# Gate and up products of the feed-forwards as 256-column products, high weights 128 bytes further on

## The reference

```python
def swiglu(x, w_in, w_out):
    gu = x @ w_in
    g, u = jnp.split(gu, 2, axis=-1)
    return (jax.nn.silu(g) * u) @ w_out
...
        x = x + 0.5 * swiglu(rms_norm(x, ffn1_norm[l]), ffn1_w_in[l], ffn1_w_out[l])
```

## Time and profile before

| | |
|---|---|
| median of 3 runs | 2235.34 us (2235.04 to 2235.49) |
| span of the profiled execution | 2233.4 us |
| around the span (median less span) | 1.9 us |
| TensorE busy | 2227.1 us, 100% of the span, granted clock 1.000 |
| VectorE busy | 1833.4 us, 82% |
| ScalarE busy | 1131.6 us, 51% |
| DMA | 53% of 16 engines' span |

### The profile page before, as it was taken

One profiled execution on the slowest core, in us unless ns is written; L12 is line 12 of the kernel. 1 busy time (PEld: TensorE's weight loads), 2 busy tenths in 40 slices (PEclk: granted clock), 3 DMA queues, 4 the chain that ended last, 5 costly groups with the idle time before them and its releaser, 6 DMA issues.

```text
span 2233.4 us, 42466 instructions
## 1 busy us (share of the span) xinstructions
PE 2227.1 (100%) x16140; PEld 2051.0 (92%) x16140; DVE 1833.4 (82%) x3023; ACT 1131.6 (51%) x1503; POOL 4.8 (0%) x10
## 2 busy tenths in 40 slices
PE   9999999999999999999999999999999999999999
PEld 8998999999998999999999889999999998999998
DVE  8888568888888668887988878888898887888887
ACT  5445465445445565444434676654454446766443
POOL 0000000000000000000000000000000000000000
PEclk9999999999999999999999999999999999999999
DMA  7555445555555435654556443555556555344654
GB/s 253 193 194 208 159 153 198 197 196 171 199 196 207 170 135 189 213 194 163 202 190 206 170 152 125 179 197 190 188 177 207 189 174 189 120 142 166 221 196 133
DMA packets 76817, 407.63 MB, mean 183 GB/s; under 512 B 9264, under 2 KB 9920, under 8 KB 44336
## 3 DMA queue, kind: packets, MB, share of 16 engines
q1 hardware_dynamic: 75792, 404.93, 53.0%
q10 hardware_dynamic: 720, 0.89, 0.1%
q0 software_dynamic: 208, 0.49, 0.1%
HBM read 405.23 MB, written 1.05 MB: 182 GB/s over the span
## 4 chain that ended last, share of the span: by engine, by line
PE 97%; DVE 1%; issue 0%; ACT 0%; DMA 0%; DVEq 0%; SPq 0%; ACTq 0%
PE ps_proj L684 13%; PE ps_aux L693 13%; PE ps_y L263 10%; PE ps_y L264 10%; PE ps_y L265 10%; PE ps_proj L688 7%; PE ps_aux L696 7%; PE ps_proj L1120 4%; PE ps_proj L1127 4%; PE ps_proj L1121 4%; PE ps_proj L263 2%; PE ps_proj L265 1%; PE ps_proj L264 1%; PE ps_aux L651 1%; PE ps_proj L651 1%; PE ps_aux L1941 1%
## 5 line engine op out<-in xcount | busy, mean ns | idle before, releaser
L130 DVE TENSOR_TENSOR w_lo_front<-w_raw_front,w_hi_front 128x2048 fp32r<-128x2048 f32 x238 | 544.0, 2286 | 42.3 <-ACT w_hi_front L105 42.0
L105 ACT CAST w_hi_front<-w_raw_front 128x2048 fp32r<-128x2048 f32 x238 | 452.9, 1903 | 178.0 <-PE ps_aux L696 144.8
L263 PE MATMUL ps_y<-hidden_lo,w_hi_back 128*128 128x256 f32 x1344 | 372.5, 277 | 0.1
L264 PE MATMUL ps_y<-hidden_hi,w_lo_back 128*128 128x256 f32 x1344 | 371.3, 276 | 0.0
L265 PE MATMUL ps_y<-hidden_hi,w_hi_back 128*128 128x256 f32 x1344 | 371.3, 276 | 0.0
L105 ACT CAST w_hi_back<-w_raw_back 128x1024 fp32r<-128x1024 f32 x248 | 259.8, 1048 | 146.4 <-PE ps_y L265 119.8
L887 ACT ACTIVATE silu_gate<-silu_gate 128x256 f32<-128x256 f32 x176 | 73.7, 419 | 508.6 <-DVE silu_gate L924 508.5
L684 PE MATMUL ps_proj<-xt_lo_hi,w_hi_front 128*128 128x512 f32 x1280 | 319.7, 392 | 0.0
L693 PE MATMUL ps_aux<-xt_lo_hi,w_hi_front 128*128 128x512 f32 x1280 | 319.6, 392 | 0.0
L130 DVE TENSOR_TENSOR w_lo_back<-w_raw_back,w_hi_back 128x1024 fp32r<-128x1024 f32 x248 | 302.2, 1218 | 4.0 <-ACT w_hi_back L105 3.3
L684 PEld LDWEIGHTS ps_proj<-xt_lo_hi,w_hi_front 128*128 128x128 f32 x1280 | 228.5, 188 | 39.6
(11 more groups left out here) (462 smaller groups left out, 3826.5 us busy)
## 6 DMA issues: line engine op xcount, KB each, us to landing
w_raw_front<-in_stream SPq DMA_DIRECT2D x251, 1024.0 KB, 4.9
w_raw_back<-in_stream SPq DMA_DIRECT2D x252, 512.0 KB, 3.7
m_rel_bias<-in_rel_bias SPq DMA_DIRECT2D x2, 2048.0 KB, 8.2
m_params<-in_params SPq DMA_DIRECT2D x2, 656.0 KB, 4.2
w_raw_front<-in_stream SPq DMA_DIRECT2D x4, 256.0 KB, 6.6
w_raw_front<-in_stream SPq DMA_DIRECT2D x2, 512.0 KB, 8.8
x<-in_x ACTq DMA_DIRECT2D x3, 256.0 KB, 6.7
out<-x SPq DMA_DIRECT2D x3, 256.0 KB, 2.3
```

Source lines behind the costliest of these rows:

```text
L105: self.nc.scalar.copy(self.hi[part][:, parity], self.raw[part][:, parity]).then_inc(self.hi_done[part], by)
L130: eng.tensor_tensor(self.lo[part][:, parity], self.raw[part][:, parity], self.hi[part][:, parity].bitcast(F32), ALU.subtract).then_inc(sel ...
L263: nc.tensor.matmul(out, ah, bl, start=start, stop=False)
L264: nc.tensor.matmul(out, al, bh, start=False, stop=False)
```

## The change

- All gate and up products have 256 columns and write the first half of their bank. A 512-column product becomes two, with the low and then the high part of the activations, each with its own load of the same 128 x 128 weights (`both_high`).
- In `ffn_up`, both gate and up are a run of 16 products on the high weights, then 8 on the low ones. PE's first wait there is now for the low weights (`split`), not for the high ones.
- In `ffn_first` and `ffn_start` the products of a block k are `all_three` (high x low, low x high, high x high) in turn.
- VectorE no longer adds halves: in a step it scales straight from PSUM; for the first slot of a feed-forward it copies the bank out (`first_out`) and scales with the rows of PSUM (`first_scale`).
- `w_hi_front` starts 128 bytes further on (the gap ahead of it has 72 floats, the gap behind it is gone). Every other buffer stays at its address.

```diff
-        sb("gap_hi_front", [P, 40], F32)
+        sb("gap_hi_front", [P, 72], F32)
         self.hi = [sb("w_hi_front", [P, 2, 2 * CH], F32R)]
-        sb("gap_hi_back", [P, 32], F32)
...
+def all_three(s, bank, part, k, stop=True):
+    hi, lo = part
+    cols = slice(k * P, (k + 1) * P)
+    out = bank[:, 0:T]
+    s.nc.tensor.matmul(out, hi[:, cols], s.xl[:, k], start=k == 0, stop=False)
+    s.nc.tensor.matmul(out, lo[:, cols], s.xh[:, k], start=False, stop=False)
+    return s.nc.tensor.matmul(out, hi[:, cols], s.xh[:, k], start=False,
+                              stop=stop and k == KD - 1)
+def both_high(s, bank, part, k, stop=False):
+    hi = part[0][:, k * P:(k + 1) * P]
+    s.nc.tensor.matmul(bank[:, 0:T], hi, s.xl[:, k], start=k == 0, stop=False)
+    return s.nc.tensor.matmul(bank[:, 0:T], hi, s.xh[:, k], start=False, stop=stop)
...
     pe = s.nc.tensor
-    gate, bank = w.parts(slot, 0), s.pj[slot % 2]
-    pe.wait_ge(w.hi_done[0], base + slot + 1)
-    for k in range(KD):
-        s.nc.tensor.matmul(bank[:], gate[0][:, k * P:(k + 1) * P],
-                           s.xlh[:, k].rearrange("p j t -> p (j t)"), start=k == 0, stop=False)
     pe.wait_ge(w.split[0], base + slot + 3)
...
+    for c, bank in enumerate((s.pj[slot % 2], s.pa[slot % 2])):
+        part = w.parts(slot, c)
+        for k in range(KD):
+            both_high(s, bank, part, k)
+        for k in range(KD):
+            last = high_low(s, bank, part, k)
+        w.taken(last, c)
...
-        for bank, part in three:
-            both_high(s, bank, part, k)
-        last_gate = high_low(s, s.pj[0], gate0, k)
+        last_gate = all_three(s, s.pj[0], gate0, k)
...
-    def add_gate(before, k):
+    def first_out(to, bank, c, done):
+        w.wait_taken(dve, base, slot0, c)
+        nc.vector.tensor_copy(to[:, 0], bank[:, 0:T]).then_inc(done, 1)
+    def first_scale(of, came, done):
+        dve.wait_ge(came, f + 1)
+        nc.vector.tensor_tensor(of[:, 0], of[:, 0], s.py[1][:, 0:T], ALU.mult).then_inc(done, 1)
+    def scale_gate(before, k):
+        p = k % 2
         w.wait_taken(dve, base + before, slot0 + k, 0)
+        nc.vector.tensor_tensor(s.act[:, p], s.pj[p][:, 0:T], s.rbc[:], ALU.mult).then_inc(
+            s.gate_scaled, 1)
```

More of the change, by code:

```diff
@@ L666, in by_high @@
     cols = slice(k * P, (k + 1) * P)
-    nc.tensor.matmul(bank[:, T:2 * T], hi[:, cols], s.xh[:, k], start=k == 0, stop=False)
+    nc.tensor.matmul(bank[:, 0:T], hi[:, cols], s.xh[:, k], start=k == 0, stop=False)
     nc.tensor.matmul(bank[:, 0:T], lo[:, cols], s.xh[:, k], start=False, stop=False)
@@ L680, in ffn_up @@
     pe = s.nc.tensor
-    gate, bank = w.parts(slot, 0), s.pj[slot % 2]
-    pe.wait_ge(w.hi_done[0], base + slot + 1)
-    for k in range(KD):
-        s.nc.tensor.matmul(bank[:], gate[0][:, k * P:(k + 1) * P],
-                           s.xlh[:, k].rearrange("p j t -> p (j t)"), start=k == 0, stop=False)
-    pe.wait_ge(w.split[0], base + slot + 3)
[L687 to L698, removed]
+    pe.wait_ge(w.split[0], base + slot + 3)
+    for c, bank in enumerate((s.pj[slot % 2], s.pa[slot % 2])):
[5 more added lines that the diff above has]
+        w.taken(last, c)
 def ffn_first(s, w, base, slot0, n):
@@ L721, in ffn_first @@
         wait_x(s, n, k)
-        for bank, part in three:
-            both_high(s, bank, part, k)
-        last_gate = high_low(s, s.pj[0], gate0, k)
-        last_up = high_low(s, s.pa[0], up0, k)
-        last = high_low(s, s.pj[1], gate1, k)
+        last_gate = all_three(s, s.pj[0], gate0, k)
+        last_up = all_three(s, s.pa[0], up0, k)
+        last = all_three(s, s.pj[1], gate1, k)
         if k == KD - 1:
@@ L768, in ffn_start @@
     gate1, up1 = w.parts(1, 0), w.parts(1, 1)
[L770 to L776, removed]
     for _ in range(WARM):
@@ L782, in ffn_start @@
         wait_x(s, 0, k)
-        high(s.pj[0], gate0, k)
+        both_high(s, s.pj[0], gate0, k)
     pe.wait_ge(s.lead_lo, 1)
     for k in range(2):
-        low(s.pj[0], gate0, k)
+        high_low(s, s.pj[0], gate0, k)
     for k in range(2, 4):
         wait_x(s, 0, k)
-        by_both(s, s.pj[0], gate0, k)
+        all_three(s, s.pj[0], gate0, k)
     pe.wait_ge(s.lead_lo, 2)
     for k in range(4):
-        by_both(s, s.pa[0], up0, k)
+        all_three(s, s.pa[0], up0, k)
     pe.wait_ge(s.lead_lo, 3)
@@ L804, in ffn_start @@
     for k in range(KD):
-        high(s.pj[1], gate1, k)
+        both_high(s, s.pj[1], gate1, k)
     pe.wait_ge(s.half_split, HALF_AT[0] + 1)
     for k in range(KD):
-        last = low(s.pj[1], gate1, k)
+        last = high_low(s, s.pj[1], gate1, k)
     w.taken(last, 0)
@@ L812, in ffn_start @@
     for k in range(KD):
-        high(s.pa[1], up1, k)
+        both_high(s, s.pa[1], up1, k)
     pe.wait_ge(s.ident_rounded, 1)
@@ L817, in ffn_start @@
     for k in range(KD):
-        last = low(s.pa[1], up1, k)
+        last = high_low(s, s.pa[1], up1, k)
     w.taken(last, 1)
@@ L913, in ffn_vector, with scale_up @@
     c0 = f * FC
-    def add_gate(before, k):
+    def first_out(to, bank, c, done):
[6 more added lines that the diff above has]
+        p = k % 2
         w.wait_taken(dve, base + before, slot0 + k, 0)
+        nc.vector.tensor_tensor(s.act[:, p], s.pj[p][:, 0:T], s.rbc[:], ALU.mult).then_inc(
+            s.gate_scaled, 1)
+    def scale_up(before, k):
         p = k % 2
[L918 to L927, removed]
-        w.wait_taken(dve, base + before, slot0 + k, 1)
[L929 to L936, removed]
+        w.wait_taken(dve, base + before, slot0 + k, 1)
+        nc.vector.tensor_tensor(s.hid[:, p], s.pa[p][:, 0:T], s.rbc[:], ALU.mult).then_inc(
+            s.up_scaled, 1)
     def hidden(before, k):
@@ L988, in ffn_vector @@
         inverse(s, n)
-    add_gate(0, 0)
-    add_up(0, 0)
+    first_out(s.act, s.pj[0], 0, s.gate_added)
+    first_out(s.hid, s.pa[0], 1, s.up_added)
     dve.wait_ge(s.rows_done, spread_count(n))
-    scale_gate(0, 0, s.py[1][:, 0:T])
-    scale_up(0, 0, s.py[1][:, 0:T])
+    first_scale(s.act, s.gate_added, s.gate_scaled)
+    first_scale(s.hid, s.up_added, s.up_scaled)
     hidden(0, 0)
```

23 lines of the change are left out of this document (4 added, 19 removed).

## The result

Before 2235.06 us, after 2238.74 us (medians of 20 executions each); the ratio, which goes by the means (2235.03 and 2239.67), is 1.0021, with a 95% interval of 1.0013 to 1.0029. I had forecast 2223.2 us and faster. One execution of after, 3706.76 us long at a lower clock, is left out of the ratio.

A forecast was written before the change was run, and what follows sets the result against it. TensorE, busy for the whole span, was taken to bound the kernel. Loops 8.5, waits 2.8 and openings 0.8 made 12.1 us off 2233.4, 2221.3, plus 1.9 for the runs' median: 2223.2 us, range 2219 to 2246.

The forecast's parts named there:

- Cost per product at the fast pace: Steady feed-forward loop: 72 narrow products at 113.33 ns make a slot 8.160 us against 8.213, 8.5 us less in all.
- third rival: All products: a fixed cost that the split doubles makes loops 6.4 us longer, 2239 us; chance 0.05, shared with small losses.
- Waits at the loops' ends: First and last down of each loop: TensorE's waits for VectorE shrink, 2.8 us saved, bounds 0 and 3.5.
- Openings: `ffn_first` and `ffn_start`: cheaper split products 0.5 us, three first downs no longer slow 0.3; 0.8 us saved.
- The wait moved ahead. ... nothing: Gate's low front weights needed 1.8 us sooner but made 6.1 us ahead, so the earlier wait costs nothing.
- Second, alignment: Reason for the fast pace in the loops: all four weight buffers now lie alike, front taking back's favourable alignment.
- Third, once fast, the streams stay fast: Reason for the fast pace in the loops: fast streams in this alignment stay fast at changes of weight buffer.
- First, the state in which the loop is entered: Reason for the fast pace: in six of eight feed-forwards the opening's restart turns fast after four slow products.
- Slow is a state that can last: Reason against the fast pace: 6 of 14 down runs restarted behind a wait stayed slow through all 24 products.
- some loops slow, 0.20: Rival: some feed-forward loops run slow, 6.6 us each; one gives 2229.8, two 2236.4, three 2243 us; chance 0.20.
- Mixers: Mixers' projections, whose front high weights move too: taken as 0 us, bounds -3 and +3.
- all loops slow: Rival: slow pace in all feed-forward loops, +44 us less the savings on waits, about 2277 us; chance 0.12.

The follow-up runs named there:

- e3: Kernel after with the low-weights wait put back behind the gate's high products and the old gaps before and behind w_hi_front: 2223.12 us, ratio 0.9945.
- e7: Kernel before with only the loop's eight wide gate and up products made 16 narrow ones, VectorE still adding halves: 2227.73 us, ratio 0.9968.
- e2: Kernel after with the old gaps, so the front's high weights 128 bytes back; waits as in after: 2229.82 us, ratio 0.9975.
- e6: Kernel after, low-weights wait back behind the high products, both low weight buffers and everything behind them 128 bytes further: 2226.81 us, ratio 0.9964.
- e4: Kernel before with only the new gaps, wide products kept: 2245.73 us, ratio 1.0047.
- e1: Kernel after with the wait for the low weights put back behind the gate's high products: 2243.73 us, ratio 1.0035.
- e5: Kernel after, low-weights wait back behind the high products, all moving operands 128 bytes further, weight buffers still alike: 2250.59 us, ratio 1.0081.
- e9: Kernel after, low-weights wait back behind the high products, both back weight buffers 128 bytes apart (modulo 512) from both front ones: 2222.20 us, ratio 0.9942.
- e10: As e3, but front's high weights 128 bytes on the other side of the other buffers, modulo 512 (gaps of 104 and 96 floats): 2223.24 us, ratio 0.9946.
- e8: As e3, but front's high weights 64 bytes from the other buffers instead of 128 (gaps of 56 and 16 floats): 2296.55 us, ratio 1.0276.

## Why the prediction was wrong

*Cost per product at the fast pace*: right. 8.160 us a slot was forecast, and 8.160 is what every fast loop shows; the loops of e3 are 8.6 us shorter than before over 19 slots each, where I had 8.5 over 20. A slow loop costs 6.5 (6.1 in these 19 slots, 0.4 in the first slot and the last down) where I had 6.6. My third rival, a fixed cost that the split doubles (2239), came near the measured time for the wrong reason: e7 doubles the products and gains 7 us. With it falls the use that I made of the Trainium skill, TensorE: Matmul & The Clock Gate, section Back-to-back issue gap, by which the split would have lost 6.4. That section gives N / 2.4 + 2.5 ns for a product by itself; for a stream of weight loads and products it gives about 81 ns at 128 columns and 131 at 512. This case's trace agrees with neither at 512 columns, with 229 ns; its 113.3 at 256 lies between the stream's two figures.

*Waits at the loops' ends*: right. I had 2.8; from before to e3 the first slot and turn give 1.9 (0.4 of it pace) and the last down 1.05. *Openings*: 0.8 forecast, none found: from before to e3 the openings and first downs together get 0.3 us longer, and six first downs of e3 are slow where three were before.

*"The wait moved ahead. ... nothing"*: this step failed first, and cost 6.7 us (e2 against e3). I read the slack of 6.1 us in the steady loop, in one slot at 610 us. A wait that is moved is moved in every turn of the loop, and in the first one there is no slack: VectorE comes out of the opening with the norm, the hidden activation and the back weights still to do, and in the profile of after the first gate starts 0.8 us after the first down is through, 1.2 in the first feed-forward and 0.4 in the fifth. The trace of before had this: its operation for the same weights ends at 363.69 too, 1.1 us behind the start of the first gate at 362.59.

*"Second, alignment"*: right where it was read, and failed where it was used. The back's high weights do lie at a good place behind a break, and the front's, moved there, turned fast in 46 of 70 runs instead of 12. But I carried this from the mixers' restarts into the loops, and called it a gain that all four buffers would lie alike. A restart at the good place still goes slow at times (24 of 70 there, two of the eight loops), and making all alike took away the one thing that ended a slow stream in the loops. The cost: in 19 executions, by their steps, 23 slow loops of 152, 1.2 an execution, so 7.9 us in the mean.

*"Third, once fast, the streams stay fast"*: right in every loop of narrow products that was profiled; not in the mixers, where e6 has a fast stream that turns slow at 324.49. *"First, the state in which the loop is entered"*: I used six restarts of one program, and the draw behind a restart changed with addresses and from one execution to the next. *"Slow is a state that can last"* stood among the reasons against, and the rival built on it (some loops slow, 0.20) was the case.

*Mixers*: I took 0 in -3 to +3; the gaps alone cost 3.0 there (e4), at the edge of it. Both parts were there: from before to after the 2172 products of the projections go from 116.2 to 115.2 ns each, 2.2 us gained where I had at most 1.7, while some 1780 products on alternating weights, the output projections above all, go from 114.3 to 116.6 ns, 4.1 us lost where I allowed 2.8. One price in the rivals is added wrong: all loops slow would be 2235.3 + 44.2 - 3.6 = 2276, not 2277.

Together: 2223.1 (e3) and 6.7 for the wait give e2, 2229.8. The profiled execution of after, less two slow loops, is 2244.1 - 13.0 = 2231.1, 1.3 more, most of it in the mixers. There the four fastest executions lie (2230.9 to 2232.5), and each slow loop adds 6.5.

What stays open: what sets the pace at a restart, why a border towards the one place frees a slow stream in the feed-forwards and 137 changes in e6's mixers do not, and why 64 bytes free none. A difference of 256 bytes was not tried, so that the places repeat every 512 bytes, and not every 256, is not shown. That the executions' steps are slow loops is shown by the profiles of after, e1 and e5 (2, 2 and 3 of them); for the other executions it is argued from the distance of 6.5 us.

## What to carry to other kernels

When a wait is moved ahead, read its slack in the first and the last turn of the loop, not in a steady one. When a long stream of equal products has two paces, look for what ends the slow one before making the stream more even; here it was, in the loops, a border between weight buffers 128 bytes apart. The best versions found (e9 at 2222.2 us, e3 and e10 at 2223.1 and 2223.2, 0.994 to 0.995 of before, their intervals overlap) keep the narrow products and such a border in every slot. What a restart does in one stage says little of a stream that has no restart. Times of single executions in steps of one size are a count of something, and the size says of what.

## What the runs showed of the hardware

A stream of 256-column fp32r products goes at 113.3 or 117.9 ns a product at the same granted clock, 1.000, without a wait in it. In the loops the pace is set within a few products of a restart and then lasts over 1300 products, through changes between weight buffers that lie alike modulo 512 bytes (after, e1, e5). With one or two buffers 128 bytes apart, modulo 512, all 40 profiled loops ended up fast (e2, e3, e6, e9, e10): slow turned to fast at 38 of 62 borders that lead to weights at a distance of 320 bytes from the moving operand, and at none of 48 that lead away from them. Where such borders come at two of three products, in the mixers of e6, a stream turned slow and stayed so for 203 products. Behind a break, projections on weights at 320 turned fast in 46 of 70 runs (after), at 192 in 12 of 70 (before), at 448 in 12 of 70 (e10). With 64 bytes between them all eight loops are slow, and the products on the buffer apart take 120 ns (e8). Wide products feel the address too: 8 x 512 columns go from a row of 2.00 us to one of 2.02 (e4).
